# Delta rule in a decoder step: the second group of heads half a chunk behind the first, and the sample chunk begun beside the last prompt chunk

## The chip, the cores and the metric

The kernel runs on one core of a Trainium2 chip. The metric is the device time of one execution in microseconds (us). Three executions of the kernel before took 2229.13 us in the median (2225.89 to 2236.6).

## The reference

One inference step of a two-layer decoder. Layer 0 is a gated delta-rule mixer with a convolutional feed-forward part, layer 1 is differential attention with the same kind of feed-forward part. There is one prompt of 512 tokens and eight sample streams of 8 tokens each. Only the delta rule concerns us here. It has 8 heads of 128 channels. Within a chunk of tokens it solves a triangular system; from chunk to chunk it hands on a state `S`:

```python
def step(S, inp):                         # one chunk; qi, ki, vi, gi (summed gates), bi (beta)
    decay = exp(where(tril, gi[:, None] - gi[None, :], -inf))
    kb = ki * bi
    lmat = where(strict, (kb @ ki.T) * decay, 0.0)
    rhs = concatenate([vi * bi, kb * exp(gi)])
    sol = triangular_solve(lmat + eye, rhs)
    u, w = sol[..., :DV], sol[..., DV:]
    v_new = u - w @ S
    attn = (qi @ ki.T) * decay
    o = (qi * exp(gi)) @ S + attn @ v_new
    S = S * exp(g_last) + (ki * exp(g_last - gi)).T @ v_new
    return S, o
```

q and k are normalised to length 1 before, and o is normalised and gated with silu(z) behind it.

## The kernel before

**Chunks and groups.** The prompt is worked in `NT` = 4 chunks of 128 tokens. The 8 heads stand in two groups of four: group 0 (A) with the tile `gA` and the PSUM banks 0 to 3, group 1 (B) with `gB` and the banks 4 to 7. The 64 sample tokens form one more chunk, folded so that it takes one group (A) alone. Each group has 16 slots of 128x512 in its tile and works a chunk in 17 rounds. A round is one batch of TensorE work (PE), and then what VectorE (DVE), ScalarE (ACT) and at three places GpSimd (POOL) make of its PSUM banks. In float32 a product of 128x128 by 128x128 shows as two records of PE. Per group and chunk there are 92 such products (4, 8 or 12 in a round), 20 transposes, and round 1.

**The rounds.** Round 1 has 8 products with one column (sums of squares), two with four columns (gate sums), one with 512 columns, and 8 transposes. Behind it stands the longest chain between two rounds: ACT loads the Ln table, takes Ln, loads the Exp table and takes three Exp; DVE makes the normalised keys and the masked decay; POOL builds three masks (`DE`, `DR`). Round 2 transposes the keys, round 3 forms q·k and k·k, rounds 4 to 12 invert the triangular matrix by doubling, round 13 combines, round 14 multiplies with the state, 15 and 16 give `v_new`, the output and the state's update, 17 turns the output.

**Order.** Every engine follows an order written out by hand, and within an engine nothing overtakes. PE begins round r of a group only when DVE and ACT have finished round r-1 of that group (`before`, L747). `turns` gives the order of the rounds over both groups: (1,A), (1,B), (2,A), (3,A), (2,B), (4,A), (3,B) and so on, B one round behind A, up to (17,B). PE, DVE and ACT all go through this list; POOL has a list of its own. A loop over the four chunks holds the list once (L873 for PE). The sample chunk follows it alone: rounds 1 to 17 of group A.

**What stands around it.** Ahead of a chunk ACT and POOL stage q, k, v, squares and the gate matrix into the slots, when `gfree` says that round 14 of the chunk before is over. When group B has finished the last prompt chunk, SP loads the eight sample states (`SS`, 4 MB, L469), which take the place of `gB`; then it writes `S` out and loads the first two blocks of the output weights. Round 14 of the sample chunk is another product than in a prompt chunk: 64 products of 128x128 by 128x16 with the loaded states (`ld_ss`), and it ends in a copy by ACT and 8 transposes. Between the last prompt chunk and the sample chunk PE makes one small product (`s_dec`) for which B must be done.

Of the kernel before, what the change touches and what calls it, by code (L numbers as in the profile page):

```python
# [22 lines left out]
P = 128  # L23
D = 1024
KB = D // P
SEQ = 512
# [3 lines left out]
T = SEQ + ST  # L30
HALF = T // 2
TD = T + ST
NT = SEQ // P
H = 8
# [29 lines left out]
C_SAME = 1280  # L64
# [23 lines left out]
def yoco_step(nc, io):  # L88
# [7 lines left out]
    with ctx:  # L96
# [507 lines left out]
        def _(pe):  # L604
# [134 lines left out]

            def delta(groups, it, sample):  # L740

                cp = C_SAMPLE if sample else C_PROMPT
                U = C[:, cp:cp + P]
                last_of = C[:, C_SAME:C_SAME + P] if sample else ones

# [5 lines left out]

                for r, g in turns(groups):
                    G = gA if g == 0 else gB
# [13 lines left out]

                    gt = (gateS if sample else small_gate(g))
                    if r == 1:
# [98 lines left out]

            def small_gate(g):
                return gtile[:, 4 * g:4 * g + 4]  # L870
# [5 lines left out]
            turned_prod = S.rearrange("p (u a) n -> p u a n", a=2)  # L876
# [231 lines left out]
        def _(dve):  # L1108
# [132 lines left out]

            def delta(groups, it, sample):
                for r, g in turns(groups):
                    if r not in R_DVE:
# [5 lines left out]
                    M = [C[:, cp + P * n:cp + P * (n + 1)] for n in range(4)]  # L1250
                    bt = betaS if sample else btile[:, 4 * g:4 * g + 4]

# [64 lines left out]
                    elif r == 17:  # L1317

                        if sample:
                            z = zT[:, :, SEQ:T].rearrange("p (u a) n -> p u a n", a=2)  # L1320
                            q = osq[:, :, SEQ:T].rearrange("p (u a) n -> p u a n", a=2)
                            for a in range(2):
                                za = z[:, :, a, :]
                                src = b[3].rearrange("p (u a n) -> p u a n", u=4, a=2)[:, :, a, :]
                                V.scalar_tensor_tensor(za, src, hgT[:, 0:1], za, ALU.mult, ALU.mult)
                                ins = copy(q[:, :, a, :], src)
                        else:
                            z = zT[:, 4 * g:4 * g + 4, bass.ds(it * P, P)]
                            V.scalar_tensor_tensor(z, u4(b[3]), hgT[:, 0:1], z, ALU.mult, ALU.mult)
                            ins = copy(osq[:, 4 * g:4 * g + 4, bass.ds(it * P, P)], u4(b[3]))  # L1330
                    ins.then_inc(out, 1)
# [4 lines left out]
            dve.wait_ge(z_act, 8)  # L1336
            with dve.Fori(0, NT) as i:
                ch.enter(DELTA_LINKS * i)
                btile = beta[:, bass.ds(i, 1), :].rearrange("p a h -> p (a h)")
                delta((0, 1), i, False)  # L1340
                ch.leave(DELTA_LINKS, NT)
            delta((0,), NT, True)
            def z_low(m):
# [258 lines left out]
        def _(act):  # L1602
# [83 lines left out]

            def delta(groups, it, sample):
                for g in groups:
                    G = gA if g == 0 else gB
                    act.wait_ge(gfree[g], it + 1)  # L1690
                    for hq, slots in ((0, ((QS, ACT.Copy), (SQQ, ACT.Square))), (H, ((SQK, ACT.Square),)),
                                      (2 * H, ((VS, ACT.Copy),))):
                        for s, fn in slots:
                            if sample:
                                src = qkvT[:, hq:hq + 8, SEQ:T]
                                dst = G[:, s, :].rearrange("p (h n) -> p h n", h=H)
                            else:
                                src = qkvT[:, hq + 4 * g:hq + 4 * g + 4, bass.ds(it * P, P)]
                                dst = u4(G[:, s, :])
                            f(dst, src, fn).then_inc(stgA[g], 1)  # L1700
                for r, g in turns(groups):
                    if r not in R_ACT:
# [40 lines left out]

            with act.Fori(0, NT) as i:
                ch.enter(DELTA_ACT * i)
                delta((0, 1), i, False)
                ch.leave(DELTA_ACT, NT)
            act.wait_ge(s_dec, 1)
            link(f(egS.rearrange("p a b -> p (a b)"), PS[:, 7, 0:64], ACT.Exp))
            delta((0,), NT, True)  # L1750

# [201 lines left out]
        def _(pool):  # L1953
# [75 lines left out]

            def delta(groups, it, sample):  # L2030
                cp = C_SAMPLE if sample else C_PROMPT
                M = [C[:, cp + P * n:cp + P * (n + 1)] for n in range(4)]
                for g in groups:
                    G = gA if g == 0 else gB
                    gt = gateS if sample else gst[g]
                    pool.wait_ge(gfree[g], it + 1)
                    take_wait()
                    if not sample:
                        copy(gst[g], gtile[:, 4 * g:4 * g + 4])
                        link(copy(bst[g], btile[:, 4 * g:4 * g + 4]))  # L2040
                    for s, hq in ((KS, H),):
                        if sample:
                            src = qkvT[:, hq:hq + 8, SEQ:T]
                            dst = G[:, s, :].rearrange("p (h n) -> p h n", h=H)
                        else:
                            src = qkvT[:, hq + 4 * g:hq + 4 * g + 4, bass.ds(it * P, P)]
                            dst = u4(G[:, s, :])
                        copy(dst, src).then_inc(stgP[g], 1)
                    mul(u4(G[:, GX, :]), bu(M[0], 4), bc(gt, P)).then_inc(stgP[g], 1)
                for r in R_POOL:  # L2050
                    for g in groups:
                        G = gA if g == 0 else gB
                        (gc, ge, ssl, rr, nbe, rqs, rqe) = gs[g]
                        bt = betaS if sample else bst[g]

                        def G4(s):
                            return u4(G[:, s, :])
                        if r == 1:
                            pool.wait_ge(gac[g], len(R_ACT) * it + 1)
                            link(mul(G4(DE), G4(DD), bc(bt, P)))  # L2060
                            link(mul(G4(DR), G4(DE), bu(M[3], 4)))
                            ins = mul(G4(DE), G4(DE), bu(M[2], 4))
                        elif r == 2:
                            mul(G4(VS), G4(VS), bc(bt, P))
                            pool.wait_ge(gdv[g], len(R_DVE) * it + 1)
                            ins = mul(G4(KD), G4(KH), bc(ge[:, 4:8], P))
                        elif r == 14:

                            pool.wait_ge(gdv[g], len(R_DVE) * it + upto(R_DVE, 14))
                            Sg = S[:, 4 * g:4 * g + 4, :]  # L2070
                            if sample:
                                pool.sem_inc(gpl[g], 1)
                                continue
                            else:
                                ins = mul(Sg, Sg, bc(ge[:, 8:12], P))
                        ins.then_inc(gpl[g], 1)
                for g in groups:
                    pool.wait_ge(gdv[g], len(R_DVE) * it + upto(R_DVE, R_FREE))
                    pool.sem_inc(gfree[g], 1)

# [5 lines left out]
            for g in range(2):  # L2086
                pool.sem_inc(gfree[g], 1)
            with pool.Fori(0, NT) as i:
                ch.enter(DELTA_POOL * i)
                gtile = gate[:, bass.ds(i, 1), :].rearrange("p a h -> p (a h)")  # L2090
                btile = beta[:, bass.ds(i, 1), :].rearrange("p a h -> p (a h)")
                delta((0, 1), i, False)
                ch.leave(DELTA_POOL, NT)
            seq16 = C[:, C_SEQ16:C_SEQ16 + 16]
            mul(gx16, bc(gateS, 16), bu(seq16, 4)).then_inc(s_gx, 1)
            delta((0,), NT, True)
            pool.wait_ge(gac[0], (NT + 1) * len(R_ACT))
# [146 lines left out]
```

## Time and profile before

| | us |
|---|---|
| median of 3 runs | 2229.13 (2225.89 to 2236.6) |
| the profiled execution, its own time | 2228.45 |
| its span | 2226.6 |
| PE busy | 1975.0 (89%) |
| DVE / ACT / POOL busy | 1049.6 / 683.2 / 887.3 |
| mean granted clock of TensorE | 0.938 of full |
| from round 1 of the first prompt chunk to the end of the sample chunk | 412.30 (278.43 to 690.73) |

The delta rule is 412.30 us of the span. Outside it PE is busy nearly all the time with the big products of the projections, the feed-forward parts and attention. The granted clock has two levels: 1.00 is 2.4 GHz and 0.50 is 1.2 GHz; a value between them is a mean over both.

### The profile page before, as it was taken

The page shows a single profiled execution, that of the slowest core. Times are in us where ns is not written, and L with a number is a line of the kernel's source. Part 1 is how long each engine was busy: PE and PEld are TensorE (multiplying, and loading weights), DVE is VectorE, ACT ScalarE, POOL GpSimd, SP SyncE. Part 2 cuts the span into 40 slices and gives each one's busy share as a digit, 9 for nine tenths or more (in the row PEclk, how much of TensorE's full clock was granted, in tenths as well). Part 3 has the DMA queues.
Part 4 walks back from the last instruction along what each step waited for, and adds up shares of the span by engine and source line. Part 5 has one row for each costly group of instructions (what it writes and reads, how often), then busy time and mean ns, then how long its engine had stood idle before and what let it go on. Part 6 is the DMA issues. An engine that isn't in the chain of part 4 may idle for free.

```text
span 2226.6 us, 38380 instructions
## 1 busy us (share of the span) xinstructions
PE 1975.0 (89%) x14780; PEld 1820.2 (82%) x14780; DVE 1049.6 (47%) x1675; ACT 683.2 (31%) x1008; POOL 887.3 (40%) x737
## 2 busy tenths in 40 slices
PE   5999777878676899999999799888887999999995
PEld 4999776877664799999999799855555999999994
DVE  3998145455426346245155532455554354253443
ACT  3444233333214234222122212144335332122220
POOL 3555223123104465456366433100004765464554
PEclk9999988997876999999999899999997999999997
DMA  4223100000300532232222133187771322222211
GB/s 116 66 76 84 44 1 0 0 0 0 89 15 19 141 87 79 76 95 85 82 70 66 61 114 105 64 308 290 289 261 48 108 85 84 86 76 85 83 50 46
DMA packets 241699, 196.75 MB, mean 88 GB/s; under 512 B 7363, under 2 KB 221509, under 8 KB 241355
## 3 DMA queue, kind: packets, MB, share of 16 engines
q1 hardware_dynamic: 233548, 166.20, 24.7%
q10 hardware_dynamic: 8064, 29.36, 3.5%
q8 instruction: 58, 0.95, 0.2%
q14 instruction: 29, 0.24, 0.0%
HBM read 183.01 MB, written 12.53 MB: 88 GB/s over the span
## 4 chain that ended last, share of the span: by engine, by line
PE 70%; DVE 13%; issue 6%; ACT 3%; POOL 3%; DMA 2%; ACTq 1%; SPq 1%; DVEq 0%; POOLq 0%
PE PS L606 66%; DVE f L1117 6%; PE PS L609 4%; DVE f L1114 2%; DVE f L1225 2%; ACT f L1608 1%; POOL f L1985 1%; ACT f L1611 1%; POOL f L1962 1%; ACTq L1886 1%; DMA f<-in_cache_k 1%; DVE f L1223 1%; DMA f<-in_a_conv_w 1%; ACT L1608 1%; DVE f L1494 1%
## 5 line engine op out<-in xcount | busy, mean ns | idle before, releaser
L606 PE MATMUL PS<-r,r 128*128 128x288 f32 (+1 forms) x10080 | 1337.6, 295 | 24.1 <-DVE r L1117 14.5
L606 PEld LDWEIGHTS PS<-r,r 128*128 128x128 f32 x10080 | 1324.5, 190 | 35.0 <-issue 15.0
L1117 DVE TENSOR_TENSOR f<-PS,f 128x512 f32<-128x512 f32 (+9 forms) x464 | 228.0, 516 | 596.4 <-PE PS L606 545.2
L1611 ACT ACTIVATE r<-f 128x1024 fp32r<-128x1024 f32 (+4 forms) x265 | 262.3, 998 | 588.0 <-PE PS L606 449.8
L2113 POOL TENSOR_TENSOR r<-f,r 128x1024 fp32r<-128x1024 f32 x128 | 311.8, 2439 | 315.6 <-ACT r L1611 315.6
L606 PE MATMUL PS<-f,f 128*32 128x256 f32 (+14 forms) x1890 | 268.5, 401 | 67.5 <-POOLq L1987 19.4
L1962 POOL TENSOR_TENSOR f<-f,f 128x512 f32<-128x512 f32 (+2 forms) x155 | 157.4, 1033 | 368.0 <-DVE f L1117 173.2
L609 PE MATMUL PS<-f,f 128*128 128x128 f32 (+5 forms) x1234 | 190.1, 299 | 108.1 <-DVE f L1117 48.2
L606 PEld LDWEIGHTS PS<-f,f 128*32 128x32 f32 (+4 forms) x1890 | 162.4, 167 | 137.3 <-issue 84.9
L609 PEld LDWEIGHTS PS<-f,f 128*128 128x128 f32 (+5 forms) x1234 | 149.1, 156 | 151.1 <-issue 74.0
L1611 ACT ACTIVATE f<-PS 128x512 f32<-128x512 f32 (+5 forms) x225 | 122.6, 562 | 421.9 <-PE PS L609 241.1
L606 PE MATMUL PS<-f 128*128 128x128 f32 x1504 | 196.1, 290 | 45.6 <-ACT f L1611 20.0
L606 PEld LDWEIGHTS PS<-f 128*128 128x128 f32 x1504 | 185.4, 203 | 55.3 <-DVE f L1117 21.7
L1992 POOL TENSOR_TENSOR r<-f,r 128x1024 fp32r<-128x1024 f32 (+1 forms) x44 | 136.7, 3116 | 228.4 <-ACT r L1611 228.0
L1114 DVE COPY f<-PS 128x512 f32<-128x512 f32 (+7 forms) x216 | 124.4, 583 | 211.4 <-PE PS L609 142.9
L1962 POOL TENSOR_TENSOR f<-f 128x1 f32<-128x1 f32 (+3 forms) x136 | 95.2, 701 | 265.5 <-PE PS L606 197.9
L1608 ACT ACTIVATE f<-f 128x512 f32 (+6 forms) x206 | 106.8, 555 | 238.6 <-DVE f L1407 176.4
L1117 DVE TENSOR_TENSOR f<-f,f 128x1 f32<-128x1 f32 (+8 forms) x116 | 113.5, 981 | 82.8 <-DMA f<-in_b_w_q 48.1
L1407 DVE SCALAR_TENSOR_TENSOR f<-f,f,f 128x592 f32<-128x592 f32 x88 | 118.7, 1349 | 3.1
L1225 DVE SCALAR_TENSOR_TENSOR f<-f,f,f 128x600 f32<-128x600 f32 x72 | 109.1, 1515 | 2.5
L1117 DVE TENSOR_TENSOR f<-f,PS 128x288 f32<-128x288 f32 (+2 forms) x144 | 53.4, 421 | 116.8 <-POOL f L1962 109.3
L2018 POOL TENSOR_TENSOR r<-f,r 128x1024 fp32r<-128x1024 f32 x24 | 65.1, 2712 | 83.7 <-ACT r L1611 83.7
(63 smaller groups left out, 689.4 us busy)
## 6 DMA issues: line engine op xcount, KB each, us to landing
f<-in_f_w_up SPq DMA_DIRECT2D x88, 512.0 KB, 3.8
f<-in_cache_k SPq DMA_DIRECT2D x64, 512.0 KB, 5.4
f<-in_cache_v ACTq DMA_DIRECT2D x56, 512.0 KB, 6.8
f<-in_a_w_in SPq DMA_DIRECT2D x32, 512.0 KB, 4.1
f<-in_f_w_down SPq DMA_DIRECT2D x32, 512.0 KB, 4.2
f<-in_w_kv SPq DMA_DIRECT2D x8, 1024.0 KB, 5.4
out<-f SPq DMA_DIRECT2D x13, 512.0 KB, 3.3
f<-in_f_w_down SPq DMA_DIRECT2D x16, 384.0 KB, 3.6
```

The source lines that it names most:

```text
L606: return nc.tensor.matmul(out, lhsT, rhs, start=start, stop=stop)
L609: return nc.tensor.transpose(out, in_, ident[0:n, 0:n])
L1114: return V.tensor_copy(out, in_)
L1117: return V.tensor_tensor(out, a, b, op)
L1225: ins = V.scalar_tensor_tensor(cv[:, 0:m], pad[:, a:a + m], tp[:, w + a:w + a + 1], cv[:, 0:m], ALU.mult, ALU.add)
L1407: ins = V.scalar_tensor_tensor(cv[:, 0:m], pad[:, a:a + m], tp[:, w + a:w + a + 1], cv[:, 0:m], ALU.mult, ALU.add)
L1608: return A.activation(out, in_, func, **kw)
L1611: return A.activation(out, in_, ACT.Copy)
L1962: return G_.tensor_tensor(out, a, b, ALU.mult)
L1992: G_.tensor_tensor(w.lo2[n], w.raw2[n], w.hi_f[n], ALU.subtract).then_inc(w_lo, 1)
L2018: G_.tensor_tensor(inW.lo2[n], inW.raw2[n], inW.hi_f[n], ALU.subtract).then_inc(w_lo, 1)
L2113: G_.tensor_tensor(upW.lo2[n], upW.raw2[n], upW.hi_f[n], ALU.subtract).then_inc(w_lo, 1)
```

## The change

`turns` goes and `skew` comes. A half chunk h pairs the front rounds of one group with the rear rounds of the other: for h = 0 rounds 9 to 17 of B (of the chunk before) with rounds 1 to 9 of A; for h = 1 rounds 10 to 17 of A with rounds 1 to 8 of B. In each pair the rear round stands first. The first chunk begins with rounds 1 to 9 of A alone. The last half h = 0 pairs B's rounds 9 to 17 of the last prompt chunk with rounds 1 to 9 of the sample chunk; its rounds 10 to 17 follow alone. The small product `s_dec` stands between them. The arithmetic of each round is as before.

```diff
-        def turns(groups):
-            if len(groups) == 1:
-                return [(r, groups[0]) for r in range(1, ROUNDS + 1)]
-            first, second = groups
-            order = [(1, first), (1, second), (2, first)]
-            for r in range(3, ROUNDS + 1):
-                order += [(r, first), (r - 1, second)]
-            return order + [(ROUNDS, second)]
+        def skew(h, it, back=None, sample=False):
+            front, rear = (0, 1) if h == 0 else (1, 0)
+            n = 9 if h == 0 else 8
+            order = []
+            for r in range(1, n + 1):
+                if back is not None:
+                    order.append((r + 18 - n - 1, rear, back[0], back[1]))
+                if it is not None:
+                    order.append((r, front, it, sample))
+            return order
...
             pe.wait_ge(gates, 1)
-            with pe.Fori(0, NT) as i:
-                gtile = gate[:, bass.ds(i, 1), :].rearrange("p a h -> p (a h)")
-                delta((0, 1), i, False)
+            delta(skew(0, 0))
+            delta(skew(1, 0, (0, False)))
+            with pe.Fori(1, NT) as i:
+                delta(skew(0, i, (i + (-1), False)))
+                delta(skew(1, i, (i, False)))
+            delta(skew(0, NT, (NT - 1, False), True))
             pe.wait_ge(s_gx, 1)
             pe.wait_ge(gdv[1], NT * len(R_DVE))
             mm(PS[:, 7, 0:64], ones, gx16.rearrange("p a b -> p (a b)")).then_inc(s_dec, 1)
-            delta((0,), NT, True)
+            delta(skew(1, None, (NT, True)))
```

DVE and ACT get the same list; ACT stages one group ahead of each half (`delta(skew(1, i, (i, False)), (1, i, False))`) in place of both ahead of a chunk. POOL's work for a chunk is cut in three:

```diff
+            def first_half(it, sample):
+                stage(0, it, sample)
+                front(0, it, sample)
+                rear(1, it + (-1), False)
+            def second_half(it):
+                stage(1, it, False)
+                front(1, it, False)
+                rear(0, it, False)
```

`stage` copies the keys and the gate matrix, `front` is POOL's work of rounds 1 and 2, `rear` that of round 14 and the release of the slots.

What this does to the order. In the pieces below `f_8192_132` is group A's tile and `f_8192_131` group B's. On PE before, in the loop over the prompt chunks, from the transposes of (1,A) to (2,A):

```order
L609 MATMUL PS<-f_2706_57,f_8192_132 128x128 x8
L606 MATMUL PS<-f_2706_57,f_8192_131 128x1 [waits o_out1,stgP1,stgA1]
L606 MATMUL PS<-f_2706_57,f_8192_131 128x1 x7
L606 ISA
L606 MATMUL PS<-f_40_71,f_2706_57 128x4 x2
L606 MATMUL PS<-f_8192_131,f_2706_57 128x512
L609 MATMUL PS<-f_2706_57,f_8192_131 128x128 x8
L750 ISA
L750 ISA [waits gdv0]
L609 MATMUL PS<-f_2706_57,f_8192_132 128x128 [waits gac0]
L609 MATMUL PS<-f_2706_57,f_8192_132 128x128 x3
```

PE after, at the same place, from the transposes of (1,A) through (10,B) and (2,A) to the first product of (11,B):

```order
L617 MATMUL PS<-f_2706_57,f_8192_132 128x128 x8
L754 REGISTER_ALU
L754 ISA [waits gdv1]
L614 MATMUL PS<-f_8192_131 128x128 [waits gac1]
L614 MATMUL PS<-f_8192_131 128x128 x7
L754 ISA
L754 ISA [waits gdv0]
L617 MATMUL PS<-f_2706_57,f_8192_132 128x128 [waits gac0]
L617 MATMUL PS<-f_2706_57,f_8192_132 128x128 x3
L754 REGISTER_ALU
L754 REGISTER_ALU [waits gdv1]
L614 MATMUL PS<-f_8192_131 128x128 [waits gac1]
```

Between round 1 and round 2 of A stood round 1 of B; now one round of 8 products of B stands there, and B's next one is behind A's round 2. On DVE after, in the loop, the end of (1,A) and the two evacuations of B that follow it, (10,B) and (11,B):

```order
L1124 TENSOR_TENSOR f_8192_132<-PS,f_8_91 128x512 [waits dve_ch]
L380 REGISTER_ALU
L1264 ISA [waits dve_ch]
L1124 TENSOR_TENSOR f_8192_132<-f_8192_132,f_4_93 128x512 [waits gac0]
L380 REGISTER_ALU
L1124 TENSOR_TENSOR f_8192_132<-f_8192_132,f_2706_57 128x512 [waits dve_ch]
L1268 REGISTER_ALU
L1121 COPY f_8192_131<-PS 128x512 [waits gpe1]
L1268 REGISTER_ALU
L1308 ISA [waits gpe1]
L1124 TENSOR_TENSOR f_8192_131<-PS,f_8192_131 128x512 [waits gdv1]
```

Behind DVE's work of (1,A) stood that of (1,B); now B's copy of round 10, for which (11,B) waits, is queued behind it.

## Rows read from the trace of the kernel before

**Rows 1.** Stretches; columns: busy us (instructions) by engine, granted clock, DMA.

```profile
278.43:357.83 79.40, 64.17 (x473) 59.37 (x474) 38.85 (x69) 28.29 (x48) 20.38 (x24) 0.86 0.00 1
357.83:435.52 77.69, 62.55 (x465) 57.73 (x465) 39.35 (x70) 26.68 (x45) 18.80 (x22) 0.87 0.00 0
435.52:513.57 78.05, 62.85 (x469) 58.05 (x469) 39.77 (x70) 27.20 (x46) 18.80 (x22) 0.89 0.00 0
513.57:597.34 83.77, 67.29 (x470) 61.72 (x470) 41.13 (x72) 25.59 (x44) 16.67 (x16) 0.83 0.02 6
597.34:642.67 45.33, 27.00 (x143) 23.40 (x143) 13.46 (x25) 8.55 (x14) 6.23 (x5) 0.67 0.47 117
642.67:690.73 48.06, 38.64 (x204) 36.38 (x204) 6.37 (x11) 5.30 (x7) 5.52 (x2) 0.63 0.00 1
```

**Rows 2.** Timeline, start of the second chunk: start, duration, engine, instruction, idle before.

```profile
357.83 5.16 PE L606 MATMUL PS<-f,f 128*128 128x1 f32 x17
...
362.79 1.92 PE L609 MATMUL PS<-f,f 128*128 128x128 f32 x8
...
364.49 3.40 PE L606 MATMUL PS<-f,f 128*128 128x1 f32 x22
...
367.73 1.46 PE L609 MATMUL PS<-f,f 128*128 128x128 f32 x8
...
370.35 2.36 DVE L1117 TENSOR_TENSOR f<-f,f 128x512 f32<-128x512 f32 x2
...
372.84 1.11 PE L609 MATMUL PS<-f,f 128*128 128x128 f32 x4 [3.65 <-DVE f L1117]
...
377.63 3.79 PE L606 MATMUL PS<-f 128*128 128x128 f32 x16 [3.67 <-ACT f L1611]
...
381.66 2.14 DVE L1117 TENSOR_TENSOR f<-PS,f 128x512 f32<-128x512 f32 x3 [1.22 <-PE PS L606]
...
383.85 1.09 PE L609 MATMUL PS<-f,f 128*128 128x128 f32 x8 [1.74 <-DVE f L1117]
...
389.90 9.99 PE L606 MATMUL PS<-f 128*128 128x128 f32 x88
```

**Rows 3.** Stretches of 2 us at the start of the second chunk; columns as in rows 1.

```profile
356.00:358.00 2.00, 1.40 (x11) 1.17 (x11) 1.12 (x2) 2.00 (x5) 1.20 (x2) 0.99 0.00 0
358.00:360.00 2.00, 2.00 (x11) 2.00 (x11) 0.75 (x2) 0.68 (x2) 0.00 (x0) 0.50 0.00 0
366.00:368.00 2.00, 2.00 (x14) 1.47 (x14) 0.32 (x2) 1.97 (x3) 0.00 (x0) 1.00 0.00 0
370.00:372.00 2.00, 0.00 (x0) 0.00 (x0) 1.83 (x3) 0.00 (x0) 1.92 (x2) 0.50 0.00 0
380.00:382.00 2.00, 2.00 (x11) 1.86 (x10) 0.78 (x2) 0.00 (x0) 2.00 (x2) 0.54 0.00 0
382.00:384.00 2.00, 0.27 (x3) 0.15 (x2) 1.73 (x3) 0.60 (x1) 2.00 (x3) 1.00 0.00 0
```

**Rows 4.** Timeline, round 1 of B at half clock, fourth chunk.

```profile
520.16 6.18 PE L606 MATMUL PS<-f,f 128*128 128x1 f32 x22
526.14 1.92 PE L609 MATMUL PS<-f,f 128*128 128x128 f32 x8
```

**Rows 5.** Timeline, the last prompt chunk's end and the sample chunk.

```profile
594.03 12.06 SPq L469 DMA_DIRECT2D f<-in_state_delta  x8
...
597.34 6.34 PE L606 MATMUL PS<-f,f 128*128 128x1 f32 x22 [2.53 <-ACT f L1608]
...
642.67 2.05 PE L606 MATMUL PS<-f 128*128 128x128 f32 x16 [2.23 <-DVE f L1297]
...
648.34 1.16 PE L606 MATMUL PS<-f 128*128 128x128 f32 x8 [0.78 <-DVE f L1117]
...
652.12 24.98 PE L606 MATMUL PS<-f,f 128*128 128x16 f32 x128 [0.69 <-ACT f L1611]
```

**Rows 6.** DMA issues from 570 to 660 us: KB each, median us to landing.

```profile
f<-in_state_delta SPq DMA_DIRECT2D x8, 512.0 KB, 7.3
```

More of the change, by code:

```diff
@@ L738, in _, with delta @@
             pe.wait_ge(tr_evac, 1)
[L740 to L744, printed above, removed]
+            def delta(order):
                 def before(g, r):
@@ L750, in before @@
                             pe.wait_ge(s, len(rounds) * it + upto(rounds, r))
-                for r, g in turns(groups):
+                for r, g, it, sample in order:
+                    cp = C_SAMPLE if sample else C_PROMPT
+                    U = C[:, cp:cp + P]
+                    last_of = C[:, C_SAME:C_SAME + P] if sample else ones
                     G = gA if g == 0 else gB
@@ L1240, in _, with delta @@
             V.memset(S, 0.0).then_inc(s_zero, 1)
-            def delta(groups, it, sample):
-                for r, g in turns(groups):
+            def delta(order):
+                for r, g, it, sample in order:
                     if r not in R_DVE:
@@ L1336, in _ @@
             dve.wait_ge(z_act, 8)
[L1337 to L1342, printed above, removed]
+            delta(skew(0, 0))
+            delta(skew(1, 0, (0, False)))
+            with dve.Fori(1, NT) as i:
+                ch.enter(DELTA_LINKS * i + (-DELTA_LINKS))
+                delta(skew(0, i, (i + (-1), False)))
+                delta(skew(1, i, (i, False)))
+                ch.leave(DELTA_LINKS, NT - 1)
+            delta(skew(0, NT, (NT - 1, False), True))
+            delta(skew(1, None, (NT, True)))
             def z_low(m):
@@ L1685, in _, with delta @@
                 f(zT[:, m, :], zT[:, m, :], ACT.Silu).then_inc(z_act, 1)
-            def delta(groups, it, sample):
-                for g in groups:
+            def delta(order, stage=None):
+                if stage is not None:
+                    g, it, sample = stage
                     G = gA if g == 0 else gB
@@ L2028, in _, with stage @@
                 low(inW, m % 2, NQ + m + 2)
-            def delta(groups, it, sample):
+            def stage(g, it, sample):
                 cp = C_SAMPLE if sample else C_PROMPT
                 M = [C[:, cp + P * n:cp + P * (n + 1)] for n in range(4)]
[L2033 to L2079, printed above, removed]
@@ new lines, in stage @@
+                G = gA if g == 0 else gB
+                gt = gateS if sample else gst[g]
+                pool.wait_ge(gfree[g], it + 1)
+                take_wait()
+                if not sample:
+                    copy(gst[g], gates_of(gate, it, g))
+                    link(copy(bst[g], gates_of(beta, it, g)))
+                if sample:
+                    src = qkvT[:, H:2 * H, SEQ:T]
+                    dst = G[:, KS, :].rearrange("p (h n) -> p h n", h=H)
+                else:
+                    src = qkvT[:, H + 4 * g:H + 4 * g + 4, one_of(it, P)]
+                    dst = u4(G[:, KS, :])
@@ new lines, in stage, with front, G4 @@
+                copy(dst, src).then_inc(stgP[g], 1)
+                mul(u4(G[:, GX, :]), bu(M[0], 4), bc(gt, P)).then_inc(stgP[g], 1)
+            def front(g, it, sample):
+                cp = C_SAMPLE if sample else C_PROMPT
+                M = [C[:, cp + P * n:cp + P * (n + 1)] for n in range(4)]
+                G = gA if g == 0 else gB
+                ge = gs[g][1]
+                bt = betaS if sample else bst[g]
+                def G4(s):
+                    return u4(G[:, s, :])
+                pool.wait_ge(gac[g], len(R_ACT) * it + 1)
+                link(mul(G4(DE), G4(DD), bc(bt, P)))
+                link(mul(G4(DR), G4(DE), bu(M[3], 4)))
+                mul(G4(DE), G4(DE), bu(M[2], 4)).then_inc(gpl[g], 1)
+                mul(G4(VS), G4(VS), bc(bt, P))
+                pool.wait_ge(gdv[g], len(R_DVE) * it + 1)
+                mul(G4(KD), G4(KH), bc(ge[:, 4:8], P)).then_inc(gpl[g], 1)
@@ L2087, in _ @@
                 pool.sem_inc(gfree[g], 1)
[L2088 to L2093, printed above, removed]
+            def second_half(it):
+                stage(1, it, False)
+                front(1, it, False)
+                rear(0, it, False)
+            stage(0, 0, False)
+            front(0, 0, False)
+            second_half(0)
+            with pool.Fori(1, NT) as i:
+                ch.enter(DELTA_POOL * i + (-DELTA_POOL))
+                first_half(i, False)
+                second_half(i)
+                ch.leave(DELTA_POOL, NT - 1)
             seq16 = C[:, C_SEQ16:C_SEQ16 + 16]
             mul(gx16, bc(gateS, 16), bu(seq16, 4)).then_inc(s_gx, 1)
-            delta((0,), NT, True)
+            first_half(NT, True)
+            rear(0, NT, True)
             pool.wait_ge(gac[0], (NT + 1) * len(R_ACT))
```

44 lines of the change are left out of this document (30 added, 14 removed).

## The prediction

> **What bounds the kernel now.** I read the stretches first [rows 1]. The delta rule takes 412.3 us: four prompt chunks of 79.4, 77.7, 78.1 and 83.8 us, then the sample chunk in 93.4 us, of which its first nine rounds take 45.3 and the rest 48.1. Nothing outside it is touched, so the whole prediction is a sum over this stretch. In the second chunk PE is busy 62.55 of 77.69 us, DVE 39.35, ACT 26.68, POOL 18.80. So PE's list is the path, and two things lengthen it: places where PE waits, and places where it works at half clock.
>
> The timeline of the chunk's start shows the waits [rows 2]. Round 1 of A begins at 357.83 and ends at 364.71 (362.79 + 1.92). DVE finishes its part of it at 372.71, and PE begins (2,A) at 372.84: 8.1 us from round 1 to round 2. In the meantime (1,B) runs, 364.49 to 369.19, so PE itself waits only 3.65 us. Another 3.67 us go ahead of (3,A), because ACT is in B's round 1, and 1.74 ahead of (4,A), behind three DVE operations of 2.14 us. The two chains of round 1 run largely side by side, once per chunk. From (4,A), at 383.85, to the next chunk at 435.52 the two groups cover each other well.
>
> The granted clock is 0.99 in the last 2 us before round 1, 0.50 in the first column products, 1.00 again in the dense end of round 1, 0.50 in the wait, and it stays low through (2,A), (3,A) and (2,B) until 382 [rows 3]. Of the two levels 0.50 is 1.2 GHz and 1.00 is 2.4 GHz.
>
> **Prices of a round.** 88 records in 9.99 us at full clock [rows 2] are 0.1135 us each, two for a product: 1.8 us for a round of eight products, 0.9 for four, 2.7 for twelve. Four transposes take 1.11 us with their tail at half clock [rows 2]; I take 0.45 for them at full clock. Round 1 takes 7.9 us at half clock (520.16 to 528.06, [rows 4]), so 4.0 at full. A group has 92 products (20.9), 20 transposes (2.2) and round 1 (4.0): about 27 us, so 54 us per chunk for both groups, before as after. No product is added or dropped.
>
> **The half chunk after the change, at full clock.** PE's list is now (9,B), (1,A), (10,B), (2,A), (11,B), (3,A) and so on, and with the groups exchanged in the other half.
>
> 1. Round 1 to round 2. The 8.1 us [rows 2] stay: ACT's two table loads and DVE's work for this group are unchanged. PE has just one rear round, 1.8 us, to do in it, and then stands at (2,A). The next rear round is behind (2,A) in PE's list. Even without that it would not be ready, for DVE's copy of (10,B) is queued behind all of DVE's work of (1,A). Wait: 6.3 us. It comes twice per chunk: 12.6. Before it was 3.65 + 3.67 = 7.3 once.
> 2. Round 3 to round 4: three DVE operations, 2.14 us plus 0.3 for PE's tail and the semaphores, with one rear round of four products (0.9) beside it: 1.6 us, twice per chunk: 3.2. Before 1.7 once.
> 3. (9,A) to (10,A): in the list nothing stands between them, since the halves meet there. The sample chunk shows this wait bare, 2.23 us [rows 5], with the tail 2.5. Once per chunk: 2.5.
> 4. The other places, where a copy or sum of 0.7 to 1.4 us on DVE or ACT is longer than the other group's round: I walked the list round by round with the durations above and get 3.1 us in one half and 2.9 in the other: 6.0.
>
> Sum: 54 + 12.6 + 3.2 + 2.5 + 6.0 = 78.3; the walk, with finer durations, gives 78.1. The same walk over the list of before gives 71.3 at full clock, and 75.9 with (1,A), (2,A), (3,A) and (2,B) at half clock, as rows 3 show them. The trace has 78.0. So the walk is 2.1 us per chunk short, in small costs between instructions, and I add 2.1 after as well.
>
> **The clock.** In the chunk of before a wait of 3.65 us was enough for 0.50 [rows 2, 3], and it took (2,A), (3,A) and (2,B), about 6 us of busy PE, to come back. The new wait is 6.3 us, with 1.8 us of dense work ahead of it and round 1's column products ahead of that. I take half clock for round 2, the rear round and round 3 behind each wait: extra 0.45 + 1.8 + 1.8 in one half and 0.45 + 0.9 + 1.8 in the other, 7.2 us; the walk hides 0.4 of it behind waits: 6.8. Bounds: nothing (the clock stays up), and round 1 at half clock too, which in the walk adds 8.2 per chunk, for A's round 1 was at half clock in rows 3.
>
> The Trainium skill bears on this ("TensorE: Matmul & The Clock Gate", section "HAM oscillation — how this bites in real kernels"): idle gaps that come back between bursts make each burst begin throttled, and the penalty is half the throttled duration. The rows agree for before. Taken at its word, the rule would charge the full 7.2 us and not 6.8, 1.6 us more over the four chunks.
>
> Period of a chunk after: 78.1 + 2.1 + 6.8 = 87.0 us.
>
> **Beginning and end.** (a) Rounds 1 to 9 of A in the first chunk now run alone. The sample chunk shows their price, with a cold start like this one: 45.3 us from round 1 to round 10 [rows 1]. (b) From (10,A) of the first chunk to round 10 of the sample chunk are four periods. The sample's nine rounds lie in the last, so 45.3 us fall away there, just what (a) adds. (c) Rounds 10 to 17 of the sample: 48.1 as before [rows 1]. (d) `s_dec` now stands ahead of round 10: 0.7. (e) The sample states. SP issued them at 594.03, when B was done, for 12.06 us [rows 5]; with 7.3 us to land for one [rows 6] the last is there some 18 us after B's end. Before, round 14 came at 652.12, 40 us later than that; it hid everything. Now B ends about 3.2 us before round 10 and rounds 10 to 13 take 9.45 (642.67 to 652.12), with (d) 13.3 us. Round 14 waits about 4.7 us. Bounds: 0, and 8 if loads and the queue are slower beside each other. ACT's copy of the product needs `S` written out; that landing lies within the 24.98 us of the product [rows 5].
>
> In the trace's terms: after = 45.3 + 4 x 87.0 + 48.1 + 0.7 + 4.7 = 446.8 against 412.3, so +34.5. ACT loads three tables per half, six per chunk in place of five; the sixth, with four staging operations, lies ahead of round 1 of B beside the wait of item 3 and costs 0.1. POOL's list is shorter in each half and not on the path. The profiled execution took 2228.45 us, 0.7 below the median of the runs; 2228.45 + 34.5 = 2263.
>
> **Rivals.** All go by the formula 2228.45 + 4 x period - 313.5; the period that breaks even is 78.4.
>
> - *The clock stays up.* For it: a rear round of another group now separates every two fronts, and there is no pair of column-product rounds in a row. Against: 3.65 us of wait sufficed before. Period 78.1 to 80.2: 2227 to 2236. Chance 0.09.
> - *The overlap pays, faster.* The mechanism: the rear rounds fill PE so well that only the work and short waits are left. For it: from (4,A) on the groups cover each other in the trace, and a front round never waits behind another front's ACT chain (the 3.67 us go). It needs the wait at round 2 to be under about 4 us where I count 6.3, so that the period is 73, by DVE's chain being shorter with one group in it. Against: (1,A)'s chain in rows 2 has no work of B in it. It gives 2228.45 + 292 - 313.5 = 2207; it decides below a period of 78.4 less 2.8, that is 75.6. Chance 0.06.
> - *Round 1 falls to half clock as well.* For it: rows 3, and the wait of 2.5 us just ahead of B's round 1. Against: dense rounds stand before A's. Period 95.2: 2296. Chance 0.10.
> - *The states bound the end:* no case of its own, since even 8 us there is within the range.
>
> **How the numbers follow.** My case, a period of 81 to 92, has chance 0.75, and 2263 is its centre. Its half-open ends are 2239 and 2283. For 8 in 10 the range reaches 2237 to 2285: it leaves out the faster case, most of the first rival and most of the third. A measurement of this kernel tells 0.5%, 11 us, from no change. Slower by more: my case, the third rival and little of the first: 0.86. Within: 0.08. Faster by more: 0.06.
>
> **What would show it.** In the profile after: waits of 6 us of PE on DVE ahead of the transposes of round 2, eight of them and one longer at the start; the granted clock at 0.5 behind each; chunk periods of 85 to 89 us; PE busy per chunk near 61 to 63 us, as before, with 24 us idle in place of 15; a wait of 3 to 8 us ahead of the 128-record product. I am wrong if these waits are under 4 us, if the clock is near 1.0 through rounds 2 and 3, or if the period is under 80. If the period fits and the time doesn't, the error is in the beginning and end.

## The result and the profile after

The changed kernel takes 2256.15 us in the median of 4 runs (2245.89 to 2264.47) against 2228.83 us for the kernel before. The ratio is 1.0122, with a 95% interval of 1.0083 to 1.0161: slower by 1.2%. The prediction was 2263 (2237 to 2285). The profiled execution is the lowest of the four, 2245.89 us, with a span of 2244.1.

The stretches after, the same cut as in [rows 1] but from (10,A) to (10,A): the lone first half, four periods, and rounds 10 to 17 of the sample chunk. Columns: busy us (instructions) of PE, PEld, DVE, ACT and POOL, granted clock, DMA share, GB/s.

```profile
277.12:324.90 47.78, 29.39 (x143) 25.68 (x143) 13.46 (x25) 10.15 (x18) 8.30 (x10) 0.62 0.00 0
324.90:407.33 82.43, 62.36 (x469) 58.95 (x469) 39.80 (x70) 25.76 (x45) 18.77 (x22) 0.90 0.00 1
407.33:491.67 84.34, 64.33 (x469) 60.48 (x469) 39.67 (x70) 25.74 (x45) 18.77 (x22) 0.88 0.00 0
491.67:574.40 82.73, 62.75 (x468) 59.33 (x469) 39.67 (x70) 25.70 (x45) 18.77 (x22) 0.90 0.00 0
574.40:656.72 82.32, 63.27 (x470) 59.65 (x470) 39.81 (x70) 24.13 (x42) 16.56 (x16) 0.88 0.02 6
656.72:712.74 56.02, 45.11 (x204) 42.50 (x204) 6.38 (x11) 5.30 (x7) 5.53 (x2) 0.51 0.37 95
```

PE is as busy in a period (62.4 to 64.3 us) as in a chunk of [rows 1] (62.6 to 67.3), and the mean clock is no lower. What grew is the idle time, from 15 or 16 us to about 20. The whole stretch takes 435.6 us in place of 412.3, so 23.3 more: 12.9 in the four periods (331.8 against 318.9 for four chunks), and 10.4 at the two ends (47.8 + 56.0 against 93.4 for the sample chunk).

The waits of PE say where. The large ones of the same stretch, before and then after; columns: who waited for whom, us in total, times, longest.

```profile
PE PS L609 <- DVE f L1117: 36.4, 19, 7.9
PE PS L606 <- ACT f L1611: 20.7, 12, 4.1
PE PS L606 <- DVE f L1117: 14.4, 14, 2.2
...
PE PS L606 <- DVE f L1297: 9.7, 9, 2.2
```

```profile
PE PS L617 <- DVE f L1124: 69.2, 23, 8.0
PE PS L614 <- DVE f L1124: 17.1, 22, 2.2
PE PS L614 <- DVE f L1304: 11.2, 5, 2.3
...
PE PS L614 <- ACT f L1622: 4.6, 7, 1.4
PE PS L614 <- DMA f<-in_state_delta: 2.1, 1, 2.1
```

Transposes (L609 before, L617 after) waiting for DVE went from 36.4 to 69.2 us; waits for ACT's copies (L1611, now L1622) fell from 20.7 to 4.6. The first are nearly all waits ahead of rounds 2 and 4, the second mostly those of (3,A) behind B's round 1 (15.1 of the 20.7). The 11.2 us on L1304 are the five seams (9,A) to (10,A).

One half in the timeline, the second one with h = 1 (round 1 of B). It answers to [rows 2].

```profile
407.33 2.05 PE L614 MATMUL PS<-f 128*128 128x128 f32 x16 [2.31 <-DVE f L1304]
409.21 3.26 PE L614 MATMUL PS<-f,f 128*128 128x1 f32 x22
...
412.31 1.81 PE L617 MATMUL PS<-f,f 128*128 128x128 f32 x8
...
413.92 2.86 PE L614 MATMUL PS<-f 128*128 128x128 f32 x16
...
419.59 2.38 DVE L1124 TENSOR_TENSOR f<-f,f 128x512 f32<-128x512 f32 x2
421.89 0.68 DVE L1124 TENSOR_TENSOR f<-PS,f 128x512 f32<-128x512 f32 x1
422.02 1.11 PE L617 MATMUL PS<-f,f 128*128 128x128 f32 x4 [5.25 <-DVE f L1124]
422.93 5.23 PE L614 MATMUL PS<-f 128*128 128x128 f32 x32
...
429.50 1.10 PE L617 MATMUL PS<-f,f 128*128 128x128 f32 x8 [1.34 <-DVE f L1124]
```

Round 1 ends at 414.12, round 2 begins at 422.02: 7.9 us, where [rows 2] have 8.1. Between them stands (11,A) alone, and then 5.25 us of nothing. The other seven waits of this kind are 6.12, 5.37, 6.08, 6.12, 5.20, 5.09 and 5.70. The sum at 421.89, for which (12,A) waits, stands on DVE right behind the two masking operations of round 1.

The clock around this wait, to set beside [rows 3]:

```profile
411.00:413.00 2.00, 2.00 (x11) 1.48 (x11) 0.00 (x0) 0.00 (x0) 0.00 (x0) 0.85 0.00 0
413.00:415.00 2.00, 2.00 (x12) 2.00 (x11) 0.77 (x5) 0.81 (x2) 0.00 (x0) 0.50 0.00 0
...
417.00:419.00 2.00, 0.00 (x0) 0.00 (x0) 0.63 (x4) 1.96 (x5) 0.29 (x1) 1.00 0.02 4
...
421.00:423.00 2.00, 0.97 (x5) 0.98 (x6) 1.57 (x2) 0.00 (x0) 1.92 (x2) 0.50 0.00 0
423.00:425.00 2.00, 2.00 (x11) 2.00 (x11) 0.03 (x1) 0.60 (x1) 2.00 (x3) 0.50 0.00 0
425.00:427.00 2.00, 2.00 (x16) 2.00 (x15) 0.66 (x1) 0.00 (x0) 0.10 (x1) 0.74 0.04 8
```

Here the clock falls twice: towards the end of round 1, behind its column products, and again in the wait, where PE has stood still since 416.8. That is so in six of the eight halves; in the other two (their round 1 at 326.8 and 493.6) it falls in the wait alone. It is back sooner than in the kernel before: by 427 here, where the trace of before has 0.50 from 358 to 364 and from 368 to about 382.

### The profile page after: what moved, and what is told of

It reads as the page before. It is cut to its first block, busy times and chain, and to the rows that moved or that the text cites. A ratio compares the mean times of both kernels' runs of the same rounds, so it can differ in the third digit from the quotient of the medians.

```text
span 2244.1 us, 38324 instructions
## 1 busy us (share of the span) xinstructions
PE 1977.3 (88%) x14780; PEld 1830.0 (82%) x14780; DVE 1049.6 (47%) x1675; ACT 677.2 (30%) x1004; POOL 883.7 (39%) x737
## 4 chain that ended last, share of the span: by engine, by line
PE 69%; DVE 14%; issue 6%; ACT 3%; POOL 3%; DMA 2%; SPq 1%; ACTq 1%; DVEq 0%; POOLq 0%
PE PS L614 65%; DVE f L1124 6%; PE PS L617 4%; DVE f L1121 2%; DVE f L1232 2%; ACT f L1619 1%; POOL f L2001 1%; POOL f L1978 1%; ACT f L1622 1%; ACT L1619 1%; ACTq L1902 1%; DVE f L1505 1%; DVE f L1230 1%; DMA f<-in_cache_k 1%; DMA f<-in_a_conv_w 1%
## 5 line engine op out<-in xcount | busy, mean ns | idle before, releaser
L1124 DVE TENSOR_TENSOR f<-PS,f 128x512 f32<-128x512 f32 (+8 forms) x464 | 227.8, 516 | 624.5 <-PE PS L614 567.6
L1622 ACT ACTIVATE r<-f 128x1024 fp32r<-128x1024 f32 (+4 forms) x265 | 262.3, 997 | 582.3 <-PE PS L614 449.6
L617 PE MATMUL PS<-f,f 128*128 128x128 f32 (+5 forms) x1234 | 191.1, 301 | 140.1 <-DVE f L1124 80.8
L614 PE MATMUL PS<-f,f 128*32 128x256 f32 (+14 forms) x1890 | 255.6, 394 | 61.3 <-POOLq L2003 18.8
L617 PEld LDWEIGHTS PS<-f,f 128*128 128x128 f32 (+5 forms) x1234 | 148.8, 155 | 179.8 <-issue 76.8
L1622 ACT ACTIVATE f<-PS 128x512 f32<-128x512 f32 (+5 forms) x225 | 122.1, 561 | 466.3 <-PE PS L617 284.2
L614 PEld LDWEIGHTS PS<-f,f 128*32 128x32 f32 (+4 forms) x1890 | 154.8, 162 | 128.1 <-issue 78.8
L614 PE MATMUL PS<-f 128*128 128x128 f32 x1504 | 213.6, 306 | 34.5 <-DVE f L1124 17.1
L614 PEld LDWEIGHTS PS<-f 128*128 128x128 f32 x1504 | 204.3, 220 | 43.4 <-DVE f L1124 22.4
L1418 DVE SCALAR_TENSOR_TENSOR f<-f,f,f 128x592 f32<-128x592 f32 x88 | 110.5, 1255 | 3.1
```

What stands on the lines that cost most here:

```text
L614: return nc.tensor.matmul(out, lhsT, rhs, start=start, stop=stop)
L617: return nc.tensor.transpose(out, in_, ident[0:n, 0:n])
L1124: return V.tensor_tensor(out, a, b, op)
L1418: ins = V.scalar_tensor_tensor(cv[:, 0:m], pad[:, a:a + m], tp[:, w + a:w + a + 1], cv[:, 0:m], ALU.mult, ALU.add)
L1622: return A.activation(out, in_, ACT.Copy)
```

## The experiments

Every kernel ran beside the kernel before on the same chip. Beside its median stands the ratio to before with its interval. The changed kernel stands at 1.0122, and its interval is wide, 0.4% or 9 us to each side: a difference from it in medians is no finer than that. A period is the time from (10,A) to (10,A) in the trace.

The traces give a second measure. The delta rule's stretch can be read in each profiled execution, from round 1 of the first chunk to the end of the sample chunk. The rest of the program is the same in all of them and still lasted between 1808.5 and 1819.8 us. So a difference of a few us between medians need not come from the delta rule.

| kernel | median, us | delta rule in its trace, us |
|---|---|---|
| before | 2228.83 | 412.3 |
| changed | 2256.15 | 435.6 |
| e1 | 2277.78 | 461.3 |
| e2 | 2255.61 | 434.9 |
| e3 | 2234.51 | 417.9 |
| e4 | 2242.6 | 429.3 |
| e5 | 2222.41 | 410.3 |
| e6 | 2225.48 | 406.3 |
| e7 | 2230.82 | 413.9 |
| e8 | 2213.33 | 406.9 |
| e9 | 2230.94 | 419.4 |
| e10 | 2244.64 | 429.8 |

**e1: the offset without the overlap.**

```diff
-            delta(skew(0, NT, (NT - 1, False), True))
+            delta(skew(0, None, (NT - 1, False)))
...
-            delta(skew(1, None, (NT, True)))
+            delta([(r, 0, NT, True) for r in range(1, ROUNDS + 1)])
```

> The changed kernel, but the sample chunk is not overlapped: B's rounds 9 to 17 of the last prompt chunk run alone, then the sample chunk alone. Theory (the half-chunk offset itself costs, and the overlap gives back what the lone first half costs): three periods of 83 us stay, the last half (rounds 9-17 of B with rounds 1-9 of the sample, about 43 us) becomes 9 rounds of B alone (about 23 us) and 9 rounds of the sample alone (47 us), so about 27 us more than the changed kernel and 50 us more than the kernel before; the wait for the states goes. Rival (the overlap is the costly part, since the sample's long round 1 stops B and the states come late): no slower than the changed kernel.

Measured: 2277.78 us, 1.0216 (1.0199 to 1.0233). That is 50 us over the kernel before and 22 over the changed one. So the offset without the overlap costs some 50 us, and starting the sample chunk early gives 22 back. The rival is out. The trace divides them, 49 there: the three periods take 249.5 us, 10 more than three mean chunks of before (79.7 each). Another 38 come from the ends: the first half (47.8 us) and the stretch from the last (10,A) to the sample chunk (69.6) are together 117.4 us, and they stand in place of one chunk. In the first of them, and in the last 29 us of the other, one group works alone.

**e2: DVE reports round 1 when the keys are there.** DVE's last two operations of round 1 (the decay mask of q·k) are not needed by round 2.

```diff
-                        link(tt(G4(KH), u4(b[2]), bc(rr[:, 0:4], P), ALU.mult))
+                        tt(G4(KH), u4(b[2]), bc(rr[:, 0:4], P), ALU.mult).then_inc(out, 1)
                         act(1)
                         link(tt(G4(DA), G4(DD), bc(rqs, P), ALU.mult))
-                        ins = tt(G4(DA), G4(DA), bu(M[1], 4), ALU.mult)
+                        link(tt(G4(DA), G4(DA), bu(M[1], 4), ALU.mult))
+                        return
```

> The changed kernel; DVE reports round 1 as done once the normalised keys are written, ahead of its two masking operations (2.4 us), which round 2 does not need. PE's wait ahead of round 2 must shrink by 2.4 us in every half. Theory (DVE's own order holds the other group: its evacuation of round 10 or 11 is still behind the two masking operations, so PE only waits one round later): total unchanged within 4 us, PE waits 2.4 us less ahead of round 2 and about 2 us more at the rear round behind it. Rival (the chain from round 1 to round 2 is itself the path): 8 x 2.4 = about 20 us faster than the changed kernel.

Measured: 2255.61 us, 1.0118 (1.01 to 1.0135), the same as the changed kernel. The half above, in e2's timeline:

```profile
412.88 2.90 PE L614 MATMUL PS<-f 128*128 128x128 f32 x16
418.57 1.11 PE L617 MATMUL PS<-f,f 128*128 128x128 f32 x4 [2.79 <-DVE f L1124]
421.96 5.32 PE L614 MATMUL PS<-f 128*128 128x128 f32 x32 [2.28 <-DVE f L1124]
```

The wait ahead of round 2 is 2.79 in place of 5.25 us, and a new one of 2.28 us stands ahead of (12,A). PE's wait was cut in two and kept its size.

**e3: the same, and the rear group's evacuation between keys and masks.**

```diff
                         tt(G4(KH), u4(b[2]), bc(rr[:, 0:4], P), ALU.mult).then_inc(out, 1)
+                        if late is not None:      # the rear round that follows in the list
+                            do_round(*late)
                         act(1)
```

> As e2, and on DVE the rear group's evacuation of round 10 or 11 stands between the keys and the two masking operations. Same operations. Theory (in-order DVE queue): now both groups can go on; the walk gives 73.3 in place of 78.0 us per chunk at full clock, so about 20 us faster than the changed kernel and about 5 us slower to 5 faster than before. Rival (the half clock is the cost, not the wait): gain under 8 us, since waits of 3 us still bring the clock down.

Measured: 2234.51 us, 1.0021 (1.0007 to 1.0034): 21 us faster than the changed kernel and than e2, and e3 differs from e2 only by the place of one DVE evacuation in each half. The rival allowed less than 8.

```profile
408.23 1.95 PE L614 MATMUL PS<-f 128*128 128x128 f32 x16
...
413.14 1.29 DVE L1124 TENSOR_TENSOR f<-PS,f 128x512 f32<-128x512 f32 x2
...
413.89 0.66 PE L617 MATMUL PS<-f,f 128*128 128x128 f32 x4 [3.71 <-DVE f L1124]
414.35 3.26 DVE L1124 TENSOR_TENSOR f<-f,f 128x512 f32<-128x512 f32 x2
...
414.56 5.46 PE L614 MATMUL PS<-f 128*128 128x128 f32 x32
```

Here (12,A) begins right behind (2,B), at 414.56, while the masks still run on DVE. Together e2 and e3 show that two things held PE in the changed kernel: the chain of round 1, and, behind it on DVE, the other group's evacuation. The early report alone gives nothing, both together give the time back; the moved evacuation without the early report was not run. e3's periods are 77.9, 76.6, 81.8 and 80.3 us, so 79.1 in the mean, over the walk's 73.3.

**e4: filler in the wait.** Ten products with an unread result ahead of each round 2.

```diff
+                    if r == 2:
+                        for _ in range(10):
+                            mm(PS[:, 6 if g == 0 else 1, 256:512], ident, C[:, C_PROMPT:C_PROMPT + 256])
```

> The changed kernel with 10 additional products of 128x128 by 128x256, whose result nobody reads, on PE ahead of each round 2, into a PSUM bank that is free there: about 4.3 us at full clock inside the wait of 6.1 us. They lengthen nothing if the clock is up; they keep PE busy. Theory (the clock costs 82.9 - 78.1 = about 5 us per chunk): period falls to 79 to 80, 12 to 18 us faster than the changed kernel, granted clock near 1.0 in rounds 2 and 3. Rival (the extra over the full-clock walk is small costs between instructions, not the clock): no change or slower, since the fillers can run past the wait when the clock is low.

Measured: 2242.6 us, 1.0055 (1.0034 to 1.0076): 13.5 us faster than the changed kernel in the medians, with more work in it. In the traces the delta rule is 6.3 us shorter. In its second half h = 1 the fillers are in the 36 records:

```profile
415.38 6.27 PE L614 MATMUL PS<-f 128*128 128x128 f32 x36
423.44 0.66 PE L617 MATMUL PS<-f,f 128*128 128x128 f32 x4 [1.80 <-DVE f L1127]
424.12 3.83 PE L614 MATMUL PS<-f 128*128 128x128 f32 x32
```

The 32 records behind round 2 take 3.83 us where they took 5.23 in the changed kernel. The periods are 83.4, 79.2, 79.3 and 81.7. In the first and the last, round 1 of B ran wholly at half clock (6.18 us for its 22 records, in place of 3.26), and the fillers gained little or nothing. The middle two are 3.8 us shorter than the changed kernel's mean of 83.0, so at least 3.8 us of a period is the clock. They still hold 1.3 and 1.6 us at half clock: the end of round 1 in one (447.2 to 452.6), rounds 2 and 3 in the other (538.6 to 545.4). Without these they would be 77.9 and 77.8, and the walk says 78.1. So nearly all that the changed kernel has above the walk is the clock.

**e5: e3 with four fillers** ahead of each round 2.

```diff
+                    if r == 2:
+                        for _ in range(4):
+                            mm(PS[:, 6 if g == 0 else 1, 256:512], ident, C[:, C_PROMPT:C_PROMPT + 256])
```

> e3 with 4 filler products of 128x256 ahead of each round 2 (1.7 us at full clock, in the wait of about 3.5 us that is left there). Theory: what e3 still pays above its walk of 73.3 us (its periods were 78 to 80) is the clock; filler returns about 3 us per chunk: 2220 to 2226, a little faster than before. Rival: the fillers are too short to hold the clock through round 1's column products: no change against e3.

Measured: 2222.41 us, 0.9965 (0.9952 to 0.9977). This version is faster than both kernels, by 0.35% against the one before. That is less than the 0.5% which the prediction took as the bound of what a measurement of this kernel can tell, though the interval excludes 1. Its periods are 80.9, 77.8, 75.5 and 75.2; in the traces its delta rule is 7.6 us shorter than e3's.

**e6: the kernel before with fillers,** seven ahead of (2,A), behind a wait for ACT's round 1, and seven ahead of (3,A).

```diff
+                    if r in (2, 3) and g == 0:
+                        if r == 2:
+                            pe.wait_ge(gac[0], len(R_ACT) * it + 1)
+                        for _ in range(7):
+                            mm(PS[:, 3, 256:512], ident, C[:, C_PROMPT:C_PROMPT + 256])
```

> The kernel before (its order unchanged) with 7 filler products of 128x256 ahead of (2,A), behind a wait for ACT's round 1 of A, and 7 ahead of (3,A), 3 us each at full clock inside waits of 3.65 us; also in the sample chunk. The walk for before is 71.3 at full clock and 75.9 with the rounds at half clock. Theory (the order of before loses 5 to 7 us per chunk to the clock): 12 to 20 us faster than before, so this order stays ahead of the half-chunk order with the same help. Rival: the clock falls at round 1's column products whatever stands behind them, and fillers at half clock outlast the wait: 0 to 10 us slower.

Measured: 2225.48 us, 0.9982 (0.9968 to 0.9996): 3.6 us faster, where I expected 12 to 20. In the second to fourth chunk round 1 of A still ran partly at half clock: its 22 records take 5.21, 3.99 and 4.10 us against 5.73, 5.52 and 5.10 before. The fillers stand behind the place where the clock first falls. Where they stand they did their work. In the fourth chunk (2,A) and (3,A) ran at full clock:

```profile
525.78 0.66 PE L609 MATMUL PS<-f,f 128*128 128x128 f32 x4
...
530.65 2.05 PE L606 MATMUL PS<-f 128*128 128x128 f32 x16 [1.19 <-ACT f L1616]
```

The second to fourth chunks last 77.2, 75.2 and 79.9 us against 78.3, 78.1 and 83.8, so 7.8 us less in all. What half clock in round 1 costs this order was not measured. Set beside e5, e6 leaves the two orders level: the intervals overlap, by the medians e5 is 3 us ahead, and in the traces e6's delta rule is the shorter, 406.3 against 410.3. So e5's gain over the kernel before does not speak for the half-chunk order.

**e7 and e8: a shorter chain in both orders.** Exp in place of Ln leaves out the normalisation of q and k and the change of ACT's table.

```diff
-                        link(f(ssl, b[0][:, 0:8], ACT.Ln, bias=eps))
+                        link(f(ssl, b[0][:, 0:8], ACT.Exp, bias=eps, scale=0.05))
```

> The changed kernel with Exp (scaled) in place of Ln in round 1, which leaves out the normalisation of q and k; ACT loads one table fewer in each round 1 (1.28 us). Theory (nine chains of round 1 stand bare on the path after the change): 8 halves plus the first, 9 x 1.28 = 11.5 us faster than the changed kernel. Rival (the chain is covered by the rear rounds): under 4 us.

> The same edit in the kernel before (it leaves out the normalisation of q and k too). Its period has one pair of chains that run side by side; the walk gives 70.0 in place of 71.3 per chunk, and the sample chunk 1.3: 5 x 1.3 = 6.5 us faster than before; B's round 1 could save two loads, then up to 12. Theory: between 5 and 12, less than in the changed kernel. Rival (the chains weigh the same in both orders): as much as in e7.

Measured: e7 2230.82 us, 1.0007 (0.9997 to 1.0016), 25 us faster than the changed kernel; e8 2213.33 us, 0.992 (0.9901 to 0.994), 16 faster than before. e7's gain is about twice what I wrote down and e8's is above its range, because both table loads of a round 1 went, not one. The loads in the stretch, in the changed kernel and in e7:

```profile
L1619 ACT ACT_TABLE_LOAD x18 | 23.1, 1283 | 0.7
```

```profile
L1619 ACT ACT_TABLE_LOAD x3 | 3.8, 1283 | 0.1
```

The 18 are two in each of the nine chains; of e7's three one is left in the first chain and two stand behind the delta rule. Two loads of 1.283 us are 2.57 us per chain: nine bare chains would be 23 us, one per chunk and one for the sample 13. Measured 25 and 16 in the medians. e7's periods fall to 78.2 in the mean, 4.7 less, near twice 2.57, which shows both chains of a period nearly bare. How much more the saving weighs in the half-chunk order is not settled. In the traces the delta rule is 21.7 us shorter in e7 and only 5.4 in e8; but e8's profiled execution is the slowest of its four (2223.54 us, the others 2207 to 2215), and in all its four chunks B's round 1 ran at half clock (6.18 us for 22 records), which before has in one.

**e9 and e10: filler in the sample's round 14 too,** added to e5 and to e6.

```diff
                                 last = mm(out, SS[:, u, hs, :], G[:, QS:KHT + 1:KHT - QS, col:col + TS])
+                                if hs % 4 == 3 and (u, hs) != (3, 15):
+                                    mm(PS[:, 6, 256:512], ident, C[:, C_PROMPT:C_PROMPT + 256])
```

> e5, and in the sample chunk's round 14 one filler product of 128x256 behind every fourth of the 64 products of 128x16 (15 of them). In the changed kernel that product takes 27.5 us at half clock; at full clock its 128 weight loads would take about 14.5 us and the fillers 6.5. Theory: 21 to 23 us in place of 27, so 4 to 6 us faster than e5: about 2217, and faster than before by 0.5%. Rival: the clock stays low there and the fillers add up to 13 us.

> e6 with the same fillers in round 14 of the sample chunk: 4 to 6 us faster than e6, so about 2220: with the same help the two orders lie within 0.3% of each other, since e3's changed DVE order is worth about as much as the offset costs.

Measured: e9 2230.94 us, 1.0014 (1.0 to 1.0027); e10 2244.64 us, 1.0068 (1.0047 to 1.009). Both lost, 9 and 19 us. e9's trace:

```profile
650.00:660.00 10.00, 10.00 (x41) 9.37 (x40) 0.00 (x0) 0.00 (x0) 0.00 (x0) 0.50 0.00 0
```

PE is busy all the time and the clock is 0.50. The 64 products with 16 columns did not bring it back, even with a product of 256 columns behind every fourth, so the fillers were pure cost, as the rival of e9 had it: 0.85 us each, 12.8 for 15 of them. In e9's trace round 14's product takes 40.3 us in place of e5's 27.5, in e10's 40.4 in place of e6's 24.9, which had begun at full clock. The medians moved by 8.5 and 19.2 us. What differs from 12.8 lies elsewhere in the traces: e9's periods are together 3.7 us shorter than e5's, with the same program there, and e10 took 4.9 us more than e6 up to round 10 of the sample chunk and 3.3 more in rounds 10 to 13, where the clock fell too. Why the clock fell at other places in these executions stays open.

## Why the prediction was right

*The wait ahead of round 2* was the step on which all rested: 6.3 us, eight times, in place of 7.3 once per chunk. Measured 5.09 to 6.12, mean 5.6. In the two halves whose rear round ran at full clock (1.95 us) the wait is 6.12. In the other six the rear round ran partly at half clock (2.25 to 3.13 us) and hid its own extra cost in the wait. e7 shows that these chains stand bare.

*The DVE queue.* "Even without that it would not be ready" was right and more than a remark: e2 shows that freeing PE's side alone is worth nothing, e3 that it is worth 21 us with DVE's side.

*Rounds 3 to 4 and the seam:* predicted 1.6 and 2.5 with tail, measured 1.34 to 1.53 and 2.31.

*The clock and the remainder,* 6.8 + 2.1 us per chunk, were mis-sized: the periods are 4.9 us over the walk, not 8.9. They came to 82.3 to 84.3 us with about 20 us idle, and the signs asked for 85 to 89 with 24 idle. The timeline's rows say which part was off. Beside their durations at full clock (3.26, 1.04, 0.66, 3.83 and 4.73 us in these traces), the rows of round 1, round 2 and the rounds behind it took 5.0, 6.8, 5.2 and 5.3 us more in the four periods, 5.6 in the mean. The slow rear rounds, 1.2 us per period, come on top and are hidden in the waits. So the clock cost 5.6 us where 6.8 were charged, and the remainder came out at minus 0.7 where 2.1 were added: that term was off by most. Taking over the 2.1 us from before was a choice that no row supported; what they stand for there stays open. Nor were the slow rounds quite those charged. In the half shown above the 32 records behind (2,B) took 5.23 us, 1.4 more than e4's 3.83, where I had charged 2.7 for them. Against that, the last part of round 1 was slow in six halves, which I had not charged.

The 7.2 us by the rule of the Trainium skill ("TensorE: Matmul & The Clock Gate", section "HAM oscillation — how this bites in real kernels") lay further from the measured 5.6 than my 6.8. That idle time between bursts brings the clock down, as the section says, the windows above agree with (1.00 at 417 to 419, 0.50 at 421 to 423, with PE idle from 416.8).

*What I read from before about the clock* was wrong in one place. I wrote that a wait of 3.65 us was enough for 0.50. In that chunk PE is busy until 369.19, and the clock was down before it stood still:

```profile
368.00:370.00 2.00, 1.19 (x7) 0.79 (x5) 0.98 (x4) 1.78 (x5) 0.64 (x1) 0.55 0.00 0
```

A mean of 0.55 over these 2 us leaves room for only the first 0.2 us at full clock. It fell behind the column products of (1,B), not in the wait. The third chunk is the one that shows a fall in a wait, with PE idle from 447.0:

```profile
448.00:450.00 2.00, 0.00 (x0) 0.00 (x0) 1.83 (x3) 0.00 (x0) 1.92 (x2) 1.00 0.00 0
450.00:452.00 2.00, 1.11 (x4) 0.72 (x4) 1.93 (x8) 0.70 (x1) 1.81 (x2) 0.53 0.00 0
```

The charge for the new wait did not suffer, since the clock did fall in all eight.

*ACT's tables.* I counted three loads per half, six per chunk. The trace has two per half, four per chunk, against five before. I had charged 0.1 us for the sixth, so nothing hung on it.

*Beginning and end* came out longer. The lone first half took 47.8 us, not 45.3: its round 6 was still at half clock. From round 10 of the sample to round 14 it took 14.9 us, 14.1 were charged. Rounds 10 to 13 ran at half clock, 12.8 in place of 9.4, and so only 2.1 us of wait were left of the 4.7; the sign for this wait, 3 to 8 us, failed.

```profile
671.64 27.46 PE L614 MATMUL PS<-f,f 128*128 128x16 f32 x128 [2.10 <-DMA f<-in_state_delta]
```

The states set this time and not the clock: in e2, e3, e4 and e7 rounds 10 to 13 took 8.8 us, the wait grew to 5.9 to 6.3 us, and round 14 still came 14.7 to 15.1 us behind round 10. The product then took 27.5 us in place of 25.0, for the clock was low from its start, where it had been up for the first 3 us before. Rounds 10 to 17 came to 56.0 against 52.8.

*The sum:* 47.8 + 331.8 + 56.0 = 435.6, predicted 446.8. The four periods are 16 us under, the ends 5 over, so part of the closeness is luck: two errors that worked against each other. The stretch grew by 23.3 us where 34.5 were predicted. Outside it the profiled execution was 5.8 us shorter than that of before, with the same program there; the runs' medians differ by 27 us, the profiles by 17. The median of 2256 lies closer to 2263 than the stretch does to its own forecast, and nothing in the prediction accounts for that.

*The rivals.* The first (the clock stays up) fails by the windows above. The second needed a wait under 4 us; the chain is as long as before, 7.9 to 8.1 us. The third (round 1 at half clock) came true in part only: its 22 first records took 3.26 us in six halves and 3.66 and 3.83 in two.

## What to carry to other kernels

When two independent chains are interleaved on in-order engines, count for each long step how many rounds of the other chain stand between its issue and its use, on every engine in turn, not on the one that waits. An offset that sets the long step of one chain against short steps of the other exposes it once per chain; side by side the two hide each other. It also leaves a lone half at each end, which here cost more than the periods did (e1). If the offset is wanted all the same (for an overlap at the end, 22 us here), publish the result that the next round needs before those that it doesn't, and put the other chain's evacuation right behind it.

## What the runs showed of the hardware

- Filler products can pay for themselves: 90 unread products of 128x256 made the changed kernel 13.5 us faster in the medians, 6.3 of them seen in the delta rule's trace (e4), and 36 made e3 12 us faster, 7.6 in the trace (e5). Among narrow products they did not: in 64 products of 16 columns with 15 fillers the clock stayed at 0.50 (e9).
- A change of ACT's table takes 1.283 us, and Ln followed by Exp makes two of them in each round 1, 2.57 us of the 4.4 that ACT works there. Without them the half-chunk order was 1.1% faster as a whole (e7).
- The changed kernel's four runs spread over 18.6 us; in the traces the periods of the same loop differ by 2 us with the place at which the clock falls. The part outside the delta rule, where no program differs, spreads over 11.3 us in the twelve traces. Which of the two explains the spread was not tested.
